# A block inversion in a delta-rule scan, moved from 64x64 blocks to 32x32 diagonal blocks on four tiles of TensorE

## The chip, the cores and the metric

One core of one Trainium2 chip runs one inference step of a hybrid backbone. The metric is device time in microseconds of one execution, the median of three runs. All data is float32 where nothing else is said.

## The reference, cut to what matters

384 tokens (128 of a prompt, 256 of a sample) go through a norm, a projection, two token mixers side by side (attention and a two-directional RWKV-7 scan), an output projection, and a mixture of 32 experts. The change touches the scan alone:

```
def step(S, xs):
    r_t, w_t, k_t, v_t, kk_t, a_t = xs
    sa = jnp.einsum("bhvk,bhk->bhv", S, kk_t)
    S = (S * w_t[:, :, None, :] - sa[..., None] * (kk_t * a_t)[:, :, None, :]
         + v_t[..., None] * k_t[:, :, None, :])
    return S, jnp.einsum("bhvk,bhk->bhv", S, r_t)
```

There are 8 heads of 64 channels and two directions, d = 0 (forwards) and d = 1 (backwards).

## The kernel before, in words

The scan is computed in chunks of HC = 64 tokens. A tile of 128 tokens holds two chunks, one in partitions 0 to 63 and one in 64 to 127. Within a chunk the recurrence is a unit triangular system of 64x64 for each head, and its inverse turns the recurrence into matmuls. Three pairs of (direction 0, direction 1) tiles are worked through one after the other; the pairs are numbered 0 to 2 here. Most work of the two directions is interleaved, and direction d owns the PSUM banks 4d to 4d+3, `bk(d, 0)` to `bk(d, 3)`.

For each pair the order is: decay and rate vectors, 32 transposes on TensorE, the Gram products (TensorE, 64x64 weights and 128 moving columns, out to all four banks), their masks into `AM` on VectorE (L1767), the product U = AM x values on TensorE (`quads` into bank 3), a piece of the attention branch's up-projection (`up_a`, 128x128 weights and 512 moving columns; two pieces in pair 0, one in pairs 1 and 2), then the inversion, then W and the product with the inverse (`s_u`), then the state steps and outputs.

The inversion keeps the inverse's transpose `XT` and the inverse `XM`, each [128, 8 heads, 64]. It starts from blocks of 2 (L1773, L1774, and the 32x32 block transposes of VectorE, L1776), and doubles the block in each of five levels, l = 1 to 5. A level is, for both directions: P = A x XM on TensorE, a masked copy of P into `PM` on VectorE (L1784), D = P x XT on TensorE, `XT` = `XT` - D on VectorE (L1788), and, in levels 1 to 4, a transpose of `XT` into `XM` (L1791). VectorE's transpose works in blocks of 32x32, which is enough up to level 4. TensorE's part is `quads`: 8 heads x 2 chunks = 16 matmuls with 64x64 weights and 64 columns, on the two diagonal 64x64 tiles of the array; a float32 matmul stands in the trace as two records on PE and two on PEld. `mm` (L719) and ScalarE's `cp` (L1243) are helpers through which most operations go.

After the last level, W (16 matmuls of 64x64, on all four 64x64 tiles) and another `quads` run on TensorE, ScalarE copies their banks (`WT`, `UV`), and VectorE computes the bonus products (L1793, L1794) and then `UU` (L1800 where a tile starts without a state, L1804 otherwise). The state steps wait for `UU`.

The work behind the scan (normalising, output projection, routing) waits for its last output, and SyncE's queue issues the experts' weights, in 1 MB pieces, once that is nearly through.

Of the kernel before, what the change touches and what calls it, by code (L numbers as in the profile page):

```python
# [74 lines left out]
HC = 64  # L75
NB = 3
# [27 lines left out]
def constants():  # L104
# [26 lines left out]
    lev = []  # L131
    for d in range(2):
        for l in range(LEVELS):
            same = (sm >> (l + 1)) == (ch >> (l + 1))
            tb, sb = (sm >> l) & 1, (ch >> l) & 1
            lev.append(same & ((sb == 0) & (tb == 1) if d == 0 else (sb == 1) & (tb == 0)))
    lev.append(sm == ch)
# [20 lines left out]
def build(nc, a, o):  # L158
    ctx = ExitStack()
    with ctx:  # L160
# [18 lines left out]
        level16 = sb("level16", [P, (2 * LEVELS + 1) * HC], U16)  # L179
        gramm = gram16[:, :].bitcast(BF16).rearrange("p (d n) -> p d n", d=2)  # L180
        levelm = level16[:, :].bitcast(BF16).rearrange("p (l n) -> p l n", n=HC)
# [71 lines left out]
        XM, XT = two(3072, HR, HC), two(3584, HR, HC)  # L253
# [3 lines left out]
        PM, GM, UV, UU = (two(6144 + i * DR, HR, HC) for i in range(4))  # L257
# [3 lines left out]
        S0D = two(6144, 4, HD)  # L261
# [95 lines left out]
        yc yo fin chain uud rsc gpn zfill chain2v qrm modrow condq routeq""".split()  # L357
# [56 lines left out]
        NP, NX = LEVELS - 1, 2 * LEVELS - 1  # L414
# [302 lines left out]
        def _(pe):  # L717
# [154 lines left out]

            def quads(out, l, r):

                for h in range(HR):
                    for b in range(2):
                        last = mm(out(h, b), l(h, b), r(h, b))
                return last
# [24 lines left out]
            bank_block = lambda bank: lambda h, b: bank[rows_of(b), h * HC:(h + 1) * HC]  # L903
            values_of = lambda j: lambda h, b: zbuf[rows_of(b), j, ZV + h * HD:ZV + (h + 1) * HD]

            for p, pair in enumerate(pairs):
# [49 lines left out]
                for d, j in pair:  # L956
                    pe.wait_ge(S["am"], 4 * (2 * p + d) + 4)
                    quads(bank_block(bk(d, 3)), blocks(AM[d], 2), values_of(j)).then_inc(s_u[d], 1)
# [12 lines left out]
                for l in range(1, LEVELS):  # L971
                    for d, j in pair:
                        pe.wait_ge(s_x[d], NX * p + 2 * l)
                        if l > 1:
                            pe.wait_ge(s_pc[d], NP * p + l - 1)
                        quads(bank_block(bk(d, 0)), blocks(AM[d], 0), blocks(XM[d])).then_inc(s_p[d], 1)
                    for d, j in pair:
                        pe.wait_ge(s_pc[d], NP * p + l)
                        quads(bank_block(bk(d, 2)), blocks(PM[d]), blocks(XT[d])).then_inc(s_d[d], 1)
# [262 lines left out]
        def _(sc):  # L1242
# [101 lines left out]
            for p, pair in enumerate(pairs):  # L1344
# [41 lines left out]
                for d, j in pair:  # L1386
                    sc.wait_ge(s_u[d], 3 * p + 2)
                    for b in range(2):
                        cp(WT[d][:, :, rows_of(b)], bk(d, b)[:, 0:4 * HC].rearrange("p (c t) -> p c t", c=4))\
                            .then_inc(s_uc[d], 1)  # L1390
                    sc.wait_ge(s_u[d], 3 * p + 3)
                    cp(flat(UV[d]), bk(d, 3)).then_inc(s_uc[d], 1)
# [108 lines left out]
        def _(ve):  # L1501
# [212 lines left out]
            idb = levelm[:, 2 * LEVELS:2 * LEVELS + 1, :].broadcast_to([P, HR, HC])  # L1714
            by_head = lambda bank: bank.rearrange("p (h t) -> p h t", h=HR)
            flat = lambda v: v.rearrange("p a b -> p (a b)")

            def both(first, second):
                first.then_inc(S["chain"], 1)
                chain[0] += 1  # L1720
                L(second)

            def start_state(p, d):

                k0 = 2 * chunk_of(0, d)
                tt(S0C[d], states[:, d, :, :], ecol[d][:, :, k0:k0 + 1].broadcast_to([P, 4, HD]), M).then_inc(S["s0p"], 1)

            for p, pair in enumerate(pairs):
# [41 lines left out]
                for d, j in pair:  # L1770
                    transposed = levelm[:, LEVELS * (1 - d):LEVELS * (1 - d) + 1, :].broadcast_to([P, HR, HC])
                    ve.wait_ge(S["am"], 4 * (2 * p + d) + 4)
                    L(tt(XT[d], AM[d][:, :, 0, :], transposed, M))  # L1773
                    tt(XT[d], idb, XT[d], SUB).then_inc(s_x[d], 1)  # L1774
                    ve.wait_ge(s_x[d], NX * p + 1)
                    ve.transpose(flat(XM[d]), flat(XT[d])).then_inc(s_x[d], 1)  # L1776

                for l in range(1, LEVELS):
                    for d, j in pair:
                        ve.wait_ge(s_p[d], NP * p + l)  # L1780
                        if l > 1:
                            ve.wait_ge(s_d[d], NP * p + l - 1)
                        m = levelm[:, LEVELS * d + l:LEVELS * d + l + 1, :].broadcast_to([P, HR, HC])
                        tt(PM[d], by_head(bk(d, 0)), m, M).then_inc(s_pc[d], 1)  # L1784
                    for d, j in pair:
                        ve.wait_ge(s_d[d], NP * p + l)
                        ve.wait_ge(s_x[d], NX * p + 2 * l)
                        tt(XT[d], XT[d], by_head(bk(d, 2)), SUB).then_inc(s_x[d], 1)  # L1788
                        if l < LEVELS - 1:
                            ve.wait_ge(s_x[d], NX * p + 2 * l + 1)  # L1790
                            ve.transpose(flat(XM[d]), flat(XT[d])).then_inc(s_x[d], 1)  # L1791

                both(*[tt(BON[d], KD[d], zr[d], M) for d in range(2)])  # L1793
# [356 lines left out]
```

## Time and profile before

| what | us |
|---|---|
| median of 3 runs | 1604.63 (1604.15 to 1606.7) |
| the profiled execution | 1607.96 |
| its span | 1606.1 |
| PE busy | 1451.2 |
| VectorE busy | 523.9 |
| scan, first pair's lora to the last output | about 275 to 478 |
| experts' loop, DMA share 1.01 | within 602 to 1560 |

A row of the timeline gives the start in the span, the time from the first start to the last end of a run of like instructions, the engine, the line and the operation. The distance from one start to the next is what bounds a run of matmuls, since they overlap: a run of n records with a duration of their own of 0.22 us and a length L has a mean distance of (L - 0.22)/(n - 1).

### The profile page before, as it was taken

Reading aid. Unit: us, or ns where it says so; the run is one execution under the profiler, and the core shown is the slowest. Engines: PE = TensorE matmul, PEld = TensorE weight load, DVE = VectorE, ACT = ScalarE, POOL = GpSimd, SP = SyncE. Lnnn points to the kernel's source line nnn. Section 1 sums busy time; section 2 is a strip of 40 time slices with the busy share of each in tenths; the row PEclk is TensorE's granted clock in tenths of the full one; section 3 lists DMA queues with packets and bytes.
Section 4 is the critical chain, followed back from the end, with each engine's and each line's share of the span. In section 5 each row is a group of like instructions: output and inputs, shape, how many; then the busy total and the mean of one; then the engine's idle time right before and its main releaser. Section 6 shows DMA issues by size and latency. Waiting matters only on the chain.

```text
span 1606.1 us, 26114 instructions
## 1 busy us (share of the span) xinstructions
PE 1451.2 (90%) x10008; PEld 690.7 (43%) x10009; DVE 523.9 (33%) x976; ACT 262.0 (16%) x514; POOL 100.1 (6%) x191
## 2 busy tenths in 40 slices
PE   4899998988977949999989999989999998998993
PEld 1677666677773443333323323323333332332331
DVE  3564644787887551111010111101101111010126
ACT  0332433231302110111110101101101111110110
POOL 1000000000001000000000000000000000000021
PEclk8899999999998959999999999999999999999997
DMA  9556835000017659999999999999999999999995
GB/s 363 207 178 242 342 125 199 2 3 10 25 48 247 245 227 403 421 421 422 421 422 421 421 422 420 422 421 421 422 421 421 422 421 421 421 421 415 421 406 189
DMA packets 97928, 510.78 MB, mean 318 GB/s; under 512 B 14752, under 2 KB 17072, under 8 KB 45160
## 3 DMA queue, kind: packets, MB, share of 16 engines
q1 hardware_dynamic: 82680, 480.08, 73.7%
q10 hardware_dynamic: 10336, 17.18, 2.9%
q0 software_dynamic: 4848, 12.59, 2.1%
q8 instruction: 50, 0.82, 0.2%
q14 instruction: 14, 0.11, 0.0%
HBM read 491.03 MB, written 22.71 MB: 320 GB/s over the span
## 4 chain that ended last, share of the span: by engine, by line
PE 64%; DMA 15%; DVE 10%; SPq 7%; issue 3%; ACT 1%; POOL 0%; DVEq 0%; ACTq 0%; POOLq 0%
PE bank L719 51%; PE bank L723 10%; SPq L596 6%; DMA ring<-w_moe_in 5%; DMA work<-w_moe_in 3%; DMA spare<-w_moe_in 3%; PE bank L726 3%; DMA zbuf<-w_ada 1%; DVE work L2068 1%; DMA work<-rows_d,dest 1%; DVE work L1788 1%; DVE work L1767 1%; DVE work L2069 1%; DVE work L1791 1%; ACT work L1243 1%
## 5 line engine op out<-in xcount | busy, mean ns | idle before, releaser
L719 PE MATMUL bank<-work 64*64 64x64 f32 (+3 forms) x5134 | 516.8, 353 | 34.8 <-DMA work<-w_moe_in 8.9
L719 PE MATMUL bank<-ring,work 128*64 128x512 f32 (+1 forms) x1376 | 353.2, 607 | 16.3 <-DMA ring<-w_moe_in 10.3
L719 PEld LDWEIGHTS bank<-work 64*64 64x64 f32 (+2 forms) x5134 | 233.8, 136 | 283.9 <-issue 232.0
L2062 DVE TENSOR_SCALAR work<-bank 128x512 f32<-128x512 f32 x39 | 27.0, 692 | 752.6 <-PE bank L719 752.6
L719 PEld LDWEIGHTS bank<-ring,work 128*64 128x64 f32 (+1 forms) x1376 | 115.4, 145 | 224.3 <-issue 192.6
L1243 ACT ACTIVATE work<-bank 128x512 f32<-128x512 f32 (+1 forms) x223 | 110.5, 513 | 540.9 <-PE bank L719 322.5
L723 PE MATMUL bank<-parts 128*128 128x512 f32 (+1 forms) x720 | 167.2, 386 | 2.9 <-DVE parts L449 2.9
L723 PEld LDWEIGHTS bank<-parts 128*128 128x128 f32 x720 | 128.5, 190 | 33.7 <-issue 5.2
L719 PE MATMUL bank<-zbuf,work 64*64 64x64 f32 (+2 forms) x966 | 126.8, 385 | 12.9 <-DMA zbuf<-w_moe_in 4.9
L1469 ACT ACTIVATE work<-work 128x512 f32<-128x512 f32 x39 | 24.6, 631 | 469.3 <-DVE work L2062 469.3
L719 PEld LDWEIGHTS bank<-zbuf,work 64*64 64x64 f32 (+2 forms) x966 | 55.5, 137 | 77.4 <-issue 59.7
L726 PE MATMUL bank<-ident,work 128*128 128x128 f32 (+1 forms) x340 | 67.1, 315 | 23.0 <-DVE work L2069 11.2
L449 DVE TENSOR_TENSOR parts<-ring,parts 128x1024 fp32r<-128x1024 f32 (+1 forms) x40 | 45.7, 1145 | 75.8 <-ACT parts L444 75.8
L726 PEld LDWEIGHTS bank<-ident,work 128*128 128x128 f32 (+1 forms) x340 | 47.6, 177 | 50.1 <-DVE work L2069 32.4
L719 PE MATMUL bank<-spare,work 128*64 128x512 f32 (+1 forms) x256 | 62.0, 563 | 3.2 <-ACT work L1243 2.2
L684 POOL TENSOR_TENSOR half<-half 128x1 f32<-128x1 f32 x38 | 7.0, 185 | 845.8 <-PE bank L726 832.9
L719 PE MATMUL bank<-first,work 128*64 128x512 f32 x208 | 53.0, 611 | 1.9 <-DMA first<-w_moe_in 1.9
L444 ACT ACTIVATE parts<-ring 128x1024 fp32r<-128x1024 f32 (+1 forms) x40 | 39.7, 994 | 76.4 <-PE bank L723 72.6
L2068 DVE TENSOR_SCALAR work<-bank 128x256 f32<-128x256 f32 x78 | 32.9, 421 | 56.7 <-PE bank L719 55.3
L671 POOL DMA_INDIRECT zbuf<-h_d,slots x39 | 41.0, 1052 | 19.8 <-issue 19.8
L719 PE MATMUL bank<-rowc 96*64 96x512 bf16 x234 | 39.9, 392 | 1.8 <-issue 1.8
L726 PEld LDWEIGHTS bank<-ident,zbuf 128*128 128x128 f32 x204 | 23.2, 148 | 37.6 <-issue 37.5
(264 smaller groups left out, 856.9 us busy)
## 6 DMA issues: line engine op xcount, KB each, us to landing
work<-w_moe_in SPq DMA_DIRECT2D x108, 1024.0 KB, 23.5
ring<-w_moe_in SPq DMA_DIRECT2D x84, 1024.0 KB, 25.5
work<-w_moe_out SPq DMA_DIRECT2D x64, 1024.0 KB, 21.0
ring<-w_moe_out SPq DMA_DIRECT2D x44, 1024.0 KB, 20.9
ring<-w_ada SPq DMA_DIRECT2D x11, 2048.0 KB, 7.4
zbuf<-w_moe_in SPq DMA_DIRECT2D x22, 1024.0 KB
first<-w_moe_in SPq DMA_DIRECT2D x21, 1024.0 KB
spare<-w_moe_in SPq DMA_DIRECT2D x21, 1024.0 KB, 23.2
```

The lines of the kernel that those rows point to most:

```text
L444: nc.scalar.activation(zpart(t, 0, n), z_quarter(t), ACT.Copy).then_inc(S["hi"], 1)
L449: eng.tensor_tensor(zpart(t, 1, n), z_quarter(t), zpart(t, 0, n), ALU.subtract)\
L596: sp.dma_start(place_of(turn_e, c), src).then_inc(s_place[(WC * turn_e + c) % NPLACE], 16)
L671: gp.indirect_dma_start(xg, None, h2_d.rearrange("t (h n) -> (t h) n", h=2), bass.IndirectOffsetOnAxis(ap=slots[:, 0:1], axis=0), bounds_c ...
L719: return pe.matmul(out, l, r, start=start, stop=stop)
L723: return pe.matmul(out, l, r, start=start, stop=stop, skip_group_check=True)
L726: return pe.transpose(out, src, ident[0:n, 0:n])
L1243: cp = lambda out, src, scale=1.0: sc.activation(out, src, ACT.Copy, scale=scale)
L1469: sc.activation(th, gl, ACT.Tanh, scale=ALPHA / 2).then_inc(S["thd"], 1)
L1767: tt(dst, bk(d, 2 * par + i).rearrange("p (c n) -> p c n", c=2), gramm[:, d:d + 1, :].broadcast_to([P, 2, 4 * HC]), M).then_inc(S["am"], 1)
L2062: ts(gl, B[0], LIMIT, None, ALU.min).then_inc(S["thd"], 1)
L2068: LL(ts(uu[:, seg], B[1][:, seg], LIMIT, -LIMIT, ALU.min, ALU.max))
```

## The change

The blocks of 32 are handled apart from the last doubling. The arrays of the inversion become [128, 8 heads, 32] (`XC`, `XM`, `PM`), with the four 32-token blocks of a tile in the four partition groups of 32. The four levels l = 1 to 4 are one loop on TensorE (`pe.Fori`) whose waits are computed from the loop's register; a burst is now `eighths`, 8 heads x 4 blocks = 32 matmuls of 32x32 weights and 32 columns, on the four diagonal 32x32 tiles. Ahead of each burst stands `hold`, a matmul with 128x32 weights and one column. The starting block comes from a second, small Gram product (`diagonal_gram`, 32 matmuls per direction) that leaves the diagonal blocks of all heads in two banks. The last level is written out as `across`: 16 matmuls of 32x32 for P and 16 for D, between the two blocks of a chunk; ScalarE copies P and writes the off-diagonal blocks of `XT` (two copies per direction), and VectorE fills the two diagonal blocks of `XT` with one masked copy.

```
+            def hold(bank):
+                mm(bank[0:32, 0:1], ident[:, 0:32], ident[:, 0:1])
+            def diagonal_gram(d):
+                for c in range(4):
+                    for par in range(2):
+                        r = rows_of(par)
+                        for q in range(4):
+                            last = mm(bk(d, 2 * par)[part(q), part(c)], BKT[d][r, 0, c, part(q)], QRT[d][r, c, 0, part(q)])
+                return last
+            def eighths(bank, l, r):
+                for h in range(HR):
+                    for q in range(4):
+                        last = mm(bank[part(q), part(h)], l(q, h), r[part(q), h, :])
+                return last
+            def across(bank, d, l, r, into):
+                for h in range(HR):
+                    for b in range(2):
+                        src, dst = 2 * b + (d if into else 1 - d), 2 * b + (1 - d if into else d)
+                        last = mm(bank[part(dst), part(h)], l(src, dst, h), r[part(src), h, :])
+                return last
...
                 for d, j in pair:
+                    pe.wait_ge(S["am"], 4 * (2 * p + d) + 2)
+                    diagonal_gram(d).then_inc(S["gdiag"], 1)
+                for d, j in pair:
                     pe.wait_ge(S["am"], 4 * (2 * p + d) + 4)
                     quads(bank_block(bk(d, 3)), blocks(AM[d], 2), values_of(j)).then_inc(s_u[d], 1)
...
-                for l in range(1, LEVELS):
+                with pe.Fori(0, SMALL - 1) as it:
                     for d, j in pair:
-                        pe.wait_ge(s_x[d], NX * p + 2 * l)
-                        if l > 1:
-                            pe.wait_ge(s_pc[d], NP * p + l - 1)
-                        quads(bank_block(bk(d, 0)), blocks(AM[d], 0), blocks(XM[d])).then_inc(s_p[d], 1)
+                        pe.wait_ge(s_x[d], 2 * it + (NX * p + 2))
+                        pe.wait_ge(s_pc[d], it + (NP * p + 1))
+                        hold(bk(d, 0))
+                        eighths(bk(d, 0), lambda q, h: AM[d][part(q), h, 0, part(q % 2)], XM[d]).then_inc(s_p[d], 1)
                     for d, j in pair:
-                        pe.wait_ge(s_pc[d], NP * p + l)
-                        quads(bank_block(bk(d, 2)), blocks(PM[d]), blocks(XT[d])).then_inc(s_d[d], 1)
+                        pe.wait_ge(s_pc[d], it + (NP * p + 2))
+                        hold(bk(d, 2))
+                        eighths(bk(d, 2), lambda q, h: PM[d][part(q), h, :], XC[d]).then_inc(s_d[d], 1)
+                for d, j in pair:
+                    pe.wait_ge(s_x[d], NX * p + 2 * SMALL)
+                    pe.wait_ge(s_pc[d], NP * p + SMALL)
+                    across(bk(d, 0), d, lambda src, dst, h: AM[d][part(src), h, 0, part(dst % 2)], XM[d], True).then_inc(s_p[d], 1)
+                for d, j in pair:
+                    pe.wait_ge(s_pc[d], NP * p + SMALL + 1)
+                    across(bk(d, 2), d, lambda src, dst, h: PM[d][part(src), h, :], XC[d], False).then_inc(s_d[d], 1)
...
                 for d, j in pair:
+                    sc.wait_ge(s_p[d], NP * p + SMALL)
+                    sc.wait_ge(s_d[d], NP * p + SMALL - 1)
+                    cp(flat(PM[d]), bk(d, 0)[:, 0:HR * QB]).then_inc(s_pc[d], 1)
+                for d, j in pair:
+                    sc.wait_ge(s_d[d], NP * p + SMALL)
+                    sc.wait_ge(s_x[d], NX * p + 2 * SMALL + 1)
+                    for b in range(2):
+                        r = slice(QB * (2 * b + d), QB * (2 * b + d + 1))
+                        cp(XT[d][r, :, QB * (1 - d):QB * (2 - d)], bk(d, 2)[r, 0:HR * QB].rearrange("p (h t) -> p h t", h=HR), -1.0)\
+                            .then_inc(s_x[d], 1)
...
-                        m = levelm[:, LEVELS * d + l:LEVELS * d + l + 1, :].broadcast_to([P, HR, HC])
+                        m = levelm[:, SMALL * d + l:SMALL * d + l + 1, :].broadcast_to([P, HR, QB])
                         tt(PM[d], by_head(bk(d, 0)), m, M).then_inc(s_pc[d], 1)
...
-                        tt(XT[d], XT[d], by_head(bk(d, 2)), SUB).then_inc(s_x[d], 1)
-                        if l < LEVELS - 1:
-                            ve.wait_ge(s_x[d], NX * p + 2 * l + 1)
-                            ve.transpose(flat(XM[d]), flat(XT[d])).then_inc(s_x[d], 1)
+                        tt(XC[d], XC[d], by_head(bk(d, 2)), SUB).then_inc(s_x[d], 1)
+                        ve.wait_ge(s_x[d], NX * p + 2 * l + 1)
+                        ve.transpose(flat(XM[d]), flat(XC[d])).then_inc(s_x[d], 1)
+                for d, j in pair:
+                    halves_of = XT[d].rearrange("p h (i t) -> p h i t", i=2)
+                    own_half = levelm[:, 2 * SMALL + 1:2 * SMALL + 3, :].unsqueeze(1).broadcast_to([P, HR, 2, QB])
+                    tt(halves_of, XC[d].unsqueeze(2).broadcast_to([P, HR, 2, QB]), own_half, M).then_inc(s_x[d], 1)
+
+                for d in range(2):
+                    ve.wait_ge(s_x[d], NX * p + 2 * SMALL + 1)
+                    ve.wait_ge(s_d[d], NP * p + SMALL)
```

## Rows read from the trace of the kernel before

**Rows 1.** The page: the queue that fetches instructions (packets, MB, share of 16 engines' span).

```profile
q8 instruction: 50, 0.82, 0.2%
```

**Rows 2.** Busy time by window: the inversions, what follows pair 0, routing, the experts.

```profile
core 0: us, PE busy (x) PEld busy (x) DVE busy (x) ACT busy (x) POOL busy (x), PEclk, DMA share, GB/s
305.00:342.00 37.00, 32.58 (x1071) 30.52 (x1071) 27.96 (x47) 3.00 (x7) 0.00 (x0) 1.00 0.01 4
345.00:358.00 13.00, 12.14 (x43) 6.52 (x44) 12.47 (x23) 6.63 (x14) 0.00 (x0) 0.87 0.01 2
562.00:602.00 40.00, 20.08 (x143) 17.15 (x141) 23.22 (x91) 4.89 (x11) 2.48 (x6) 0.58 0.60 229
620.00:1540.00 920.00, 879.51 (x4084) 304.19 (x4084) 113.52 (x226) 106.51 (x225) 57.03 (x146) 0.98 1.01 421
```

**Rows 3.** Timeline of levels 1 and 2 in pair 0, from level 1's first burst.

```profile
305.69 4.02 PE L719 MATMUL bank<-work 64*64 64x64 f32 x128
...
310.32 1.15 PE L719 MATMUL bank<-work 64*64 64x64 f32 x32 [0.60 <-DVE work L1791]
...
311.64 3.09 PE L719 MATMUL bank<-work 64*64 64x64 f32 x96 [0.17 <-DVE work L1791]
312.83 0.69 DVE L1784 TENSOR_TENSOR work<-bank,level 128x512 f32<-128x512 f32 x1 [0.63 <-PE bank L719]
313.77 0.69 DVE L1788 TENSOR_TENSOR work<-work,bank 128x512 f32<-128x512 f32 x1 [0.24 <-PE bank L719]
314.49 0.71 DVE L1791 STREAM_TRANSPOSE work<-work 128x512 f32<-128x512 f32 x1
315.12 0.65 DVE L1788 TENSOR_TENSOR work<-work,bank 128x512 f32<-128x512 f32 x1
315.26 1.15 PE L719 MATMUL bank<-work 64*64 64x64 f32 x32 [0.53 <-DVE work L1791]
315.81 0.71 DVE L1791 STREAM_TRANSPOSE work<-work 128x512 f32<-128x512 f32 x1
316.45 0.69 DVE L1784 TENSOR_TENSOR work<-bank,level 128x512 f32<-128x512 f32 x1
316.57 3.09 PE L719 MATMUL bank<-work 64*64 64x64 f32 x96 [0.17 <-DVE work L1791]
```

**Rows 4.** Timeline: operations of 128x256 on VectorE in pair 0's state steps.

```profile
340.18 0.42 DVE L1821 TENSOR_TENSOR work<-work,smallc 128x256 f32<-128x256 f32 x1
340.52 0.42 DVE L1816 TENSOR_TENSOR work<-bank,work 128x256 f32<-128x256 f32 x1
340.98 0.43 DVE L1821 TENSOR_TENSOR work<-work,smallc 128x256 f32<-128x256 f32 x1
```

**Rows 5.** Timeline of PE: a run on all four 64x64 tiles, and the next.

```profile
340.29 0.74 PE L719 MATMUL bank<-work 64*64 64x64 f32 x34
340.82 0.33 PE L719 MATMUL bank<-zbuf,work 64*64 64x64 f32 x4
```

**Rows 6.** Timeline of pair 1 from its Gram products to its first level.

```profile
360.89 3.72 PE L719 MATMUL bank<-work 64*64 64x128 f32 x128
362.13 4.88 DVE L1767 TENSOR_TENSOR work<-bank,gram 128x512 f32<-128x512 f32 x8 [2.00 <-PE bank L719]
...
364.68 1.15 PE L719 MATMUL bank<-zbuf,work 64*64 64x64 f32 x32
...
367.07 1.15 PE L719 MATMUL bank<-zbuf,work 64*64 64x64 f32 x32 [1.24 <-DVE work L1767]
...
368.14 3.70 PE L719 MATMUL bank<-ring,first 128*128 128x512 f32 x8
...
370.42 0.71 DVE L1776 STREAM_TRANSPOSE work<-work 128x512 f32<-128x512 f32 x1
...
371.68 1.04 PE L726 MATMUL bank<-ident,work 128*64 128x128 f32 x8
...
372.65 4.03 PE L719 MATMUL bank<-work 64*64 64x64 f32 x128
```

**Rows 7.** Timeline of pair 0 from level 5's first burst to UU.

```profile
325.13 1.15 PE L719 MATMUL bank<-work 64*64 64x64 f32 x32 [0.53 <-DVE work L1791]
...
329.59 0.69 DVE L1788 TENSOR_TENSOR work<-work,bank 128x512 f32<-128x512 f32 x1 [0.32 <-PE bank L719]
330.17 0.66 ACT L1243 ACTIVATE work<-bank 128x256 f32<-128x256 f32 x2 [23.77 <-PE bank L719]
...
332.84 0.88 DVE L1800 TENSOR_SCALAR work<-work 64x512 f32<-64x512 f32 x2
```

## The prediction on record

> **What bounds the kernel now.** I read the windows first [rows 2]. In the experts' loop the DMA share is 1.01 at 421 GB/s: that stage takes what its bytes take. The weights' queue is opened by the work behind the scan, so a microsecond gained or lost in the scan moves the whole loop and the end by one. In the windows of the scan the DMA share is 0.01 and neither PE nor VectorE is full (32.6 and 28.0 of 37 us): there the two wait for each other, and a price has to be read from the timeline.
>
> In the timeline of a level [rows 3] the first burst of a level starts at 310.32, then at 315.26: a period of 4.94. It is a ring. VectorE starts D of direction 0 at 313.77 and ends the transpose of direction 1 at 315.81 + 0.71 = 316.52: 2.75 us, four operations on 128x512. PE starts 0.05 later (316.57) with P of direction 1, then D of direction 0: the same two bursts started at 311.64, and their result is used at 313.77, so 2.13 for two, which is 2 x 0.94 and 0.25 of latency after the last. 2.75 + 0.05 + 2.13 = 4.93. PE waits 0.53 and 0.17 in this ring: it is near to being the bound. Level 1 takes 310.32 - 305.69 = 4.63. Four levels take 19.45 in a pair.
>
> **What VectorE saves.** All its operations of the inversion go from 128x512 to 128x256. Such operations take 0.42, 0.46 to a dependent one and 0.34 to an independent one [rows 4]. No transpose of 128x256 is in the trace; between nothing saved (0.71) and the same ratio I take the ratio, 0.44, since its 512 takes what an arithmetic one takes. The four operations become 0.46 + 0.36 + 0.44 + 0.44 = 1.70: 1.05 less in the ring.
>
> **What TensorE pays.** A burst goes from 16 matmuls to 32, that is from 32 PE records to 64, and before each stands `hold`. All turns on the distance between records, call it r. Quads run at (1.15 - 0.22)/31 = 30 ns on two tiles [rows 3], Gram products with 128 columns at (364.68 - 360.89)/128 = 29.6 ns on four [rows 6], and a run of 64 columns on four tiles at (340.82 - 340.29)/34 = 15.6 ns [rows 5]. Times the tiles that is 60, 118 and 62 ns for a record on its own tile: it goes with the columns. By that a record of 32 columns takes 30 to 35 ns on its tile, with four tiles in turn r = 8 to 9. But no row shows records closer than 15.6 ns, so whether they can be issued so close is unknown: the bounds are 7.5 (62/8) and 30 (no better than quads). I take 9, the tile's own time, as the 15.6 is itself explained by the tiles; a burst is then 64 x 9 = 0.58 instead of 0.94. A change from 64x64 to 128x128 work costs about 0.11 (last start at 368.00, next at 368.14, where the step had been 0.03) [rows 6]; I charge the same on the way back and 0.06 for `hold`'s own two records: 0.3 per burst, 0.15 where PE stood idle anyway (bounds 0.1 and 0.4).
>
> The Trainium skill (TensorE: Matmul & The Clock Gate, Back-to-back issue gap) puts a floor of about 25 ns under the distance of small matmuls. By it a burst would be 1.6 us and this change a loss; the 15.6 ns of the four-tile run disagrees with it.
>
> **The new ring.** 1.70 (VectorE) + 0.05 + 0.15 + 0.58 (P of direction 1) + 0.3 + 0.58 (D of direction 0) + 0.25 = 3.61. The loop's branch and its computed waits are in no row; below nothing, above one fetched block of instructions per turn, 0.2% x 16 x 1606 / 50 = 1.0 us [rows 1]; I take 0.1, since a block's code is there from the turn before. 3.71 against 4.94: -1.23, in levels 2 to 4: -3.7. Level 1 starts with all bursts in a row: 0.73 + 0.88 + 0.88, then 0.25, 0.90 of VectorE and 0.05: 3.69, with the branch 3.8 against 4.63: -0.8.
>
> **Ahead of the loop.** VectorE's starting blocks shrink from 2.1 us a direction to about 1.2, but that gains nothing: in pair 1 its last transpose is done at 371.13 and PE starts level 1 at 372.65, since it is busy with `up_a` and state transposes [rows 6]. PE does pay: the diagonal Gram of direction 1 waits for the sixth mask (362.13 + 6 x 0.61 = 365.8) and `quads` for U of direction 0, now done by 365.8 beside the masks, comes behind it. 0.05 + 64 records (0.6) + 0.95 + 0.95 ends at 368.4 to 368.6, against 368.0: +0.6 (bounds +0.3 and, at 30 ns, +1.9). Behind it wait `up_a` and the loop, so all of it shows.
>
> **The last level.** Before, from its first burst at 325.13 to W's start is about 4.2 (D of direction 0 is done at 329.27, as the other direction's follows at 329.59), and to `UU` 7.7 [rows 7]. After: P bursts of 32 records on two tiles (at 16 ns 0.5), copy by ScalarE (0.33 each [rows 7] and 0.25 of latency), D bursts (0.5), two copies of ScalarE: P of direction 1 starts at 0.85, ends 1.35, is copied at 1.95; D of direction 0 is out at about 2.05, its two copies at 2.7, W at 2.75. That is 1.4 sooner; at 30 ns per record 0.4. The bonus products of VectorE may start at 2.7, against 5.1, so they don't hold `UU` up. VectorE's copy of the diagonal halves (2 x 0.69) lies beside P and D. I take -1.2.
>
> **Sum.** 3 x (+0.6 - 0.8 - 3.7 - 1.2) = 3 x -5.1 = -15. Against the profiled execution, 1607.96 (1.9 us outside the span), that is 1593; it is 3.3 above the median of the runs, so for the median 1604.6 - 15 = 1590.
>
> **Rivals.**
> 1. TensorE becomes the bound, by the distance of its records. A burst costs C = 64 r + 0.3. Once C is over 1.2 (D of direction 1 is then longer than VectorE's way from D to the next P), the ring is 4 C. At r = 15.6, the closest row, C = 1.3 and the level 5.2, with the branch 5.3: +0.37 in three levels, +0.5 in level 1, +1.0 ahead, -1.0 at the end: +1.6 per pair, +5 in all, 1609. The sign turns at about 14.5 ns. For it: that row is the fastest there is, and 30 ns looks like a habit of all 64x64 runs. Against: each row is explained by columns over tiles. In the middle, at 12 ns: C = 1.07, ring 1.2 + 3.2 + 0.1 = 4.5, and with the rest about -2 per pair, 1598.
> 2. The four tiles of a burst don't overlap because all four row groups write to one bank. Serially a record of 512 columns takes 0.44 (8 in 371.68 - 368.14) [rows 6], 0.86 ns per column, so 32 columns 28 ns: a burst of 1.8, C = 2.1, a level 8.5, 3.6 over today's: with level 1 (+3.8) and the prelude (+1.9) some +16 per pair, +47, 1650. Against it: two row groups of `quads` share a bank and run at 30 ns, where serial work would need 55.
> The Trainium skill (TensorEngine Tiling (Array Packing), Restrictions and Gotchas) says that different row tiles cannot access the same PSUM bank simultaneously; it would give this rival, and by the 30 ns of `quads` the trace does not agree.
> 3. The loop's edge costs a fetched block each time: 1.0 instead of 0.1 on 12 turns [rows 1], +11: about 1601, little or no change. Against it: the experts' loop fetches next to nothing and runs at the DMA's pace.
> 4. The granted clock falls. It is 1.00 in the inversions, 0.87 after the state steps and 0.58 in routing, where PE is busy half of the time [rows 2]. PE stays busy for 3 of 3.7 us in the new ring, so I give it little; at half clock a tile's record takes twice as long, r = 17, and a level 5.6: +10, 1614.
>
> **How the numbers follow.** No change is within 0.2% of the median, 3.2 us, about what a measurement of this kernel can tell. r up to about 10.5: 0.50 (1584 to 1594, faster). r of 11 to 13.5: 0.15 (1594 to 1601, mostly faster). r of 14 to 16: 0.15 (1602 to 1610, same or slower). One bank, or a floor of 25 ns or more (a level of 7.6, +36): 0.08. The loop's edge: 0.07, same or slightly faster. Clock: 0.05. Faster 0.62, same 0.13, slower 0.25. The range takes in the first three and the third rival: 1583 to 1609; the likeliest case alone spans 1584 to 1594.
>
> **What the changed profile would show.** Burst to burst: `eighths` as 64 records of 32*32 in 0.6 to 0.8 us, with a `hold` of 128*32 about 0.15 before; a run of 1.0 or 1.9 means rival 1 or 2. VectorE's masks at 0.42 and its transposes at 0.44. A level period of 3.7; PE idle before P of direction 0 and of direction 1 for 0.1 to 0.4 (none: PE is the bound). `up_a` 0.6 later behind the masks. W of each pair about 5 us sooner after its Gram. A stage behind the scan with the same lengths, and experts' weights issued 15 us sooner. The prediction fails if records of 32x32 keep 14.5 ns or more, if the transposes don't shrink (+0.6 a level at most), or if each turn of the loop stalls.

## The result, and the profile after

The changed kernel takes 1618.1 us (median of 7 runs, 1613.05 to 1624.99) against 1604.63 (7 runs, 1603.75 to 1606.7): ratio 1.0084, 95% interval 1.0060 to 1.0109. It is slower by 0.8%, and outside the range that was given. Its runs also spread four times as wide, and the longer ones have the lower mean granted clock (0.938 at 1613.05, 0.930 at 1624.99). The profiled execution took 1618.1, its span is 1616.1 (before: 1606.1). The medians are 13.5 us apart and the spans only 10.0, mostly because before's profiled execution lay 3.3 us above its own median.

The page after: span, instructions, clock by slice, and the queue that fetches instructions ([rows 1] before: 50 packets). A packet is 0.77 MB / 47, 16 KB.

```profile
span 1616.1 us, 30228 instructions
...
PEclk7799999888967968999999999999999999999997
...
q8 instruction: 47, 0.77, 0.2%
```

TensorE and VectorE in pair 0, from level 1's first burst on, which answers to [rows 3]:

```profile
308.04 0.22 PE L723 MATMUL bank<-ident 128*32 128x1 f32 x2
...
308.19 0.75 PE L723 MATMUL bank<-work 32*32 32x32 f32 x64
...
308.88 0.22 PE L723 MATMUL bank<-ident 128*32 128x1 f32 x2
308.99 0.42 DVE L1843 TENSOR_TENSOR work<-bank,level 128x256 f32<-128x256 f32 x1 [7.75 <-PE bank L723]
...
310.70 0.44 PE L723 MATMUL bank<-work 32*32 32x32 f32 x29
311.12 0.45 DVE L1849 STREAM_TRANSPOSE work<-work 128x256 f32<-128x256 f32 x1
...
312.97 0.74 PE L723 MATMUL bank<-work 32*32 32x32 f32 x35 [1.83 <-issue]
...
313.86 0.26 PE L723 MATMUL bank<-ident 128*32 128x1 f32 x2
...
314.05 1.07 PE L723 MATMUL bank<-work 32*32 32x32 f32 x64
```

Three things are to be seen. A burst at first is what was forecast: 64 records in (0.75 - 0.22)/63 = 8.4 ns each. In the fourth burst, after 29 of its 64 records, TensorE stands still for 1.83 us and waits for nothing that a semaphore shows. And behind the stop the same burst takes 1.07 instead of 0.75. The windows of the same stretch (columns as in [rows 2]; the clock is the number ahead of the DMA share) say why: the granted clock has gone to 0.50, the 1.2 GHz level.

```profile
308.00:310.00 2.00, 2.00 (x151) 1.83 (x153) 0.60 (x2) 0.60 (x1) 0.00 (x0) 1.00 0.00 0
310.00:312.00 2.00, 1.14 (x95) 0.97 (x90) 1.12 (x3) 0.00 (x0) 0.00 (x0) 1.00 0.04 8
312.00:314.00 2.00, 0.88 (x37) 0.76 (x37) 0.25 (x1) 0.00 (x0) 0.00 (x0) 0.53 0.00 0
314.00:316.00 2.00, 2.00 (x124) 1.91 (x127) 1.04 (x3) 0.00 (x0) 0.00 (x0) 0.50 0.00 0
...
334.00:336.00 2.00, 2.00 (x60) 2.00 (x58) 1.22 (x2) 0.97 (x3) 0.00 (x0) 0.50 0.00 0
336.00:338.00 2.00, 2.00 (x76) 1.98 (x71) 0.55 (x2) 1.44 (x4) 0.00 (x0) 1.00 0.03 8
```

It stays there for 24 us, with TensorE busy nearly all the time. The other two pairs show the same: a stop in the fourth burst of the loop's first turn, and half the clock behind it (380.4 to 390.6 and again 397.4 to 400.9 in pair 1, 445.2 to 472.5 in pair 2). Their stops:

```profile
381.28 0.43 PE L723 MATMUL bank<-work 32*32 32x32 f32 x13 [2.20 <-issue]
...
448.14 0.87 PE L723 MATMUL bank<-work 32*32 32x32 f32 x48 [4.21 <-issue]
```

The levels of pair 1, where the clock comes back just ahead of the last turn: a level of 391.83 - 386.95 = 4.88, mostly at 1.2 GHz, and one of 395.40 - 391.83 = 3.57 at 2.4 GHz.

```profile
386.95 0.26 PE L723 MATMUL bank<-ident 128*32 128x1 f32 x2 [0.18 <-issue]
...
391.83 0.22 PE L723 MATMUL bank<-ident 128*32 128x1 f32 x2 [0.36 <-DVE work L1849]
...
395.40 7.58 PE L723 MATMUL bank<-work 32*32 32x32 f32 x272 [0.16 <-DVE work L1849]
```

The second fall in pair 1 comes without a stop. From 391.0 to 397.4 the clock is at 1.00, TensorE is busy for 5.74 of 6.40 us, and it waits for 0.36 us at most. In the levels before it is busy for 12.71 of 15 us (310 to 325) and the clock stays at 1.00.

```profile
392.00:394.00 2.00, 2.00 (x174) 1.89 (x175) 1.23 (x3) 0.00 (x0) 0.00 (x0) 1.00 0.00 0
394.00:396.00 2.00, 1.84 (x143) 1.65 (x129) 1.52 (x5) 0.00 (x0) 0.00 (x0) 1.00 0.00 0
396.00:398.00 2.00, 1.86 (x92) 1.68 (x88) 1.35 (x3) 1.26 (x4) 0.00 (x0) 0.86 0.00 0
```

Where the time went, change against before in us, by the starts of the parts in the two timelines (level 1 is from its first burst to level 2's; the last level from its first burst to `UU`):

| part | forecast, 3 pairs | pair 0 | pair 1 | pair 2 | measured, sum |
|---|---|---|---|---|---|
| prelude: first mask to first burst | +1.8 | +1.3 | +0.4 | +1.0 | +2.7 |
| level 1 | -2.4 | +1.2 | +1.5 | +3.6 | +6.3 |
| levels 2 to 4 | -11.1 | +0.1 | -1.3 | -0.1 | -1.3 |
| last level to `UU` | -3.6 | -0.2 | -1.0 | +1.7 | +0.5 |
| ahead of the masks and behind `UU` | 0 | +0.6 | -1.3 | -0.2 | -0.8 |

But for rounding the sum is +7.3, and the scan went from 200.7 to 208.0. With +1.3 ahead of the scan and +2.6 between the scan and the experts' weights (there too products run at the lower clock), the weights are issued 11.2 later and the span is 10.0 longer. In pair 1 before has a dip of the clock at 347 to 350, which after does not have; its masks start 1.6 sooner behind the pair's start, and that is the -1.3.

### The profile page after: what moved, and what is told of

It reads as the page before. It is cut to its first block, busy times and chain, and to the rows that moved or that the text cites. A ratio compares the mean times of both kernels' runs of the same rounds, so it can differ in the third digit from the quotient of the medians.

```text
span 1616.1 us, 30228 instructions
## 1 busy us (share of the span) xinstructions
PE 1462.3 (90%) x12024; PEld 700.7 (43%) x12025; DVE 497.5 (31%) x976; ACT 268.6 (17%) x532; POOL 99.8 (6%) x191
## 4 chain that ended last, share of the span: by engine, by line
PE 65%; DMA 15%; SPq 8%; DVE 7%; issue 3%; ACT 1%; POOL 0%; DVEq 0%; ACTq 0%; POOLq 0%
PE bank L723 52%; PE bank L727 10%; SPq L600 7%; DMA ring<-w_moe_in 5%; DMA spare<-w_moe_in 3%; DMA work<-w_moe_in 3%; PE bank L730 3%; DMA zbuf<-w_ada 1%; DVE work L2133 1%; DMA work<-rows_d,dest 1%; DVE work L2134 1%; DVE work L1824 1%; ACT work L1286 1%; DVE ring L2146 0%; DMA rows_d<-work 0%
## 5 line engine op out<-in xcount | busy, mean ns | idle before, releaser
L723 PE MATMUL bank<-work 32*32 32x32 f32 (+5 forms) x7054 | 522.9, 322 | 35.2 <-issue 8.3
L723 PEld LDWEIGHTS bank<-work 32*32 32x32 f32 (+4 forms) x7054 | 233.9, 138 | 283.1 <-issue 242.1
L1286 ACT ACTIVATE work<-bank 128x256 f32<-128x256 f32 (+3 forms) x241 | 117.4, 502 | 550.0 <-PE bank L723 325.5
```

What stands on the lines that cost most here:

```text
L723: return pe.matmul(out, l, r, start=start, stop=stop)
L1286: cp = lambda out, src, scale=1.0: sc.activation(out, src, ACT.Copy, scale=scale)
```

## The experiments

Two theories for the stop: F, the code isn't there (it comes in blocks, and TensorE uses them up faster than they arrive), against L, the loop's branch and computed waits. Two for the clock: G, the stop alone makes it fall and it takes its time, against H, the 32x32 work does not keep the clock up or bring it back, stop or not.

**1. Levels written out.**

```
-                with pe.Fori(0, SMALL - 1) as it:
+                for it in range(SMALL - 1):
```

> The changed kernel with its four equal levels written out instead of a loop on TensorE, nothing else. In the changed kernel PE stood still for 1.83, 2.20 and 4.21 us in the fourth burst of the first turn of each loop, 458 to 502 instructions after its head. Theory F (the code arrives in blocks of 16 KB, 256 instructions, and PE, which now uses one up in 1.2 us, outruns it): written out, every block is outrun, 8 blocks a pair at some 3 us each, levels of 6 us or more, no faster than the changed kernel: 1618 to 1630 us. Rival L (the loop's branch or its register waits cause the stop): no stops in the bursts, and some 3 us less per pair: 1605 to 1610 us.

Measured: 1643.4 us, ratio 1.0243 (1.0226 to 1.0260). TensorE in pair 0:

```profile
312.12 0.47 PE L723 MATMUL bank<-work 32*32 32x32 f32 x34 [1.56 <-issue]
...
315.82 0.75 PE L723 MATMUL bank<-work 32*32 32x32 f32 x39 [1.33 <-issue]
...
319.55 0.84 PE L723 MATMUL bank<-work 32*32 32x32 f32 x43 [1.12 <-issue]
...
323.53 0.86 PE L723 MATMUL bank<-work 32*32 32x32 f32 x48 [1.38 <-issue]
...
327.26 0.95 PE L723 MATMUL bank<-work 32*32 32x32 f32 x52 [1.12 <-issue]
```

From one resumption to the next there are 126 to 128 matmul records, so with their weight loads about 256 instructions, and in these rows 3.7 to 4.0 us (3.3 to 4.1 over the three pairs, once 5.2). Without a stop the same number of records takes 2.3 us at half clock, since a burst with its `hold`, 66 records, takes 1.20. A packet of 16 KB over 256 instructions is 64 bytes for each. This is F: code comes in blocks of 256 instructions, one per some 3.7 us, which is 14.5 ns per instruction and 29 ns per record as the closest spacing that a long stretch of such code kept. `quads` of 64x64 at 30 ns per record [rows 3] just doesn't outrun it. L is refuted: without a loop the waits of this kind between 300 and 510 us are 28, 30.2 us in all, against 12 and 10.4 with it. The size was missed: 1618 to 1630 was expected.
By the Trainium skill (Runtime: NRT & Kernel Launch, Instruction fetch mechanics) code comes in 16 KiB blocks of 256 instructions, which these rows bear out. The Trainium skill says in the same section that the fetch is hidden by the sequencer's own pace; the stops of 1.1 to 1.6 us show that this does not hold here.

**2. The loop's code moved against the blocks.** The loop's head is put at slot 210 of a block.

```
-                with pe.Fori(0, SMALL - 1) as it:
+                with nc.Fori(0, SMALL - 1, engines=[mybir.EngineType.PE], head_slot={mybir.EngineType.PE: 210}) as it:
```

> The changed kernel with the loop's first instruction put at slot 210 of a block of 256, so that the body (about 550 instructions) crosses a block's edge 46, 302 and 558 instructions in: the first crossing is made while PE's queue still works on the up-projection, and the third is not reached. Theory F: the stop in the first turn goes or shrinks below 0.5 us in all three pairs, 8 us in all. For the clock, which was 0.50 for 24, 10 and 27 us after these stops: theory G (a stop lets the clock fall) expects 1.00 throughout and levels of 3.6 us, in all 1588 to 1595 us; theory H (bursts on 32x32 tiles do not keep the clock up by themselves) expects it to fall all the same and 1605 to 1612 us. Rival L expects the stops to stay where they are.

Measured: 1615.74, ratio 1.0088 (1.0057 to 1.0118), no different from the changed kernel. The stop moved with the code: in every pair it now stands behind 15 of the 64 records of the third burst, about where the expectation had the second edge (302 instructions in). It is shorter, 1.15, 1.40 and 1.84 us, but not below 0.5 as was expected:

```profile
308.90 0.62 PE L723 MATMUL bank<-work 32*32 32x32 f32 x49 [1.15 <-issue]
```

F again for the place, with the size missed. The clock is still at 0.50 from 311 to 335 in pair 0, and for 17.1 and 23.9 us in the others (10.2 and 27.3 in the changed kernel): a shorter stop spared little or nothing of that, and the time is above both that were expected.

**3. The loop and `hold` alone, at 64x64.** The kernel before, with all its five levels as one loop and `hold` ahead of each burst.

```
-                for l in range(1, LEVELS):
+                with pe.Fori(0, LEVELS - 1) as it:
...
+                        hold(bk(d, 0))
                         quads(bank_block(bk(d, 0)), blocks(AM[d], 0), blocks(XM[d])).then_inc(s_p[d], 1)
```

> The kernel before with its five levels as one loop on TensorE, with the same computed waits and a hold ahead of each burst, all on 64x64 tiles as it was. Theory F: a body of 272 instructions at 15 ns each takes a block in 3.8 us, so no stop above 0.3 us; the hold costs 0.45 in each ring of 4.94, about +7 us in 15 levels: 1609 to 1613 us, clock 1.00. Rival L: stops of 2 us in each first turn and a clock of 0.5 behind them: 1620 us or more.

Measured: 1612.24, ratio 1.0062 (1.0045 to 1.0079), as expected.

```profile
310.21 0.22 PE L719 MATMUL bank<-ident 128*32 128x1 f32 x2 [0.38 <-DVE work L1798]
...
311.44 0.22 PE L719 MATMUL bank<-ident 128*32 128x1 f32 x2
...
315.59 0.22 PE L719 MATMUL bank<-ident 128*32 128x1 f32 x2 [0.39 <-DVE work L1798]
```

A burst with its `hold` takes 1.23 where `quads` alone takes 0.94, so `hold` and the two changes of shape cost 0.3, as the prediction charged, and the ring is 5.38 instead of 4.94. No stop and no loss of clock anywhere in the levels: the loop does neither.

**4. A stop without 32x32 work.** The kernel before, in which VectorE repeats a masked copy in level 1 two, three and six times, so that TensorE waits 1.31, 2.04 and 4.21 us in pairs 0, 1 and 2.

```
+                        if l == 1 and d == 0:
+                            for _ in range((2, 3, 6)[p]):
+                                L(tt(PM[d], by_head(bk(d, 0)), m, M))
                         tt(PM[d], by_head(bk(d, 0)), m, M).then_inc(s_pc[d], 1)
```

> The kernel before (64x64 bursts, no loop), with VectorE repeating the first masked copy of level 1 two, three and six times in pairs 0, 1 and 2, so that PE stands still for about 1.4, 2.2 and 4.3 us in level 1; what is computed is the same. Theory G (a stop lets the clock fall, whatever the matmuls): the clock goes to 0.50 after at least the two longer stops. Theory H (it is the 32x32 work that does not hold or regain the clock): here, with 64x64 bursts behind, it stays at 1.00 or is back within 5 us, against 10 to 27 us in the changed kernel. Time: 7.5 us of stops and what the clock costs, 1612 to 1620 us.

Measured: 1613.3 (one run). The windows of pair 1:

```profile
376.00:378.00 2.00, 0.09 (x2) 0.09 (x4) 1.93 (x4) 0.00 (x0) 0.00 (x0) 1.00 0.61 131
378.00:380.00 2.00, 2.00 (x52) 2.00 (x54) 1.17 (x3) 0.00 (x0) 0.00 (x0) 0.69 0.00 0
380.00:382.00 2.00, 2.00 (x42) 1.99 (x40) 1.69 (x3) 0.00 (x0) 0.00 (x0) 0.50 0.03 8
382.00:384.00 2.00, 2.00 (x66) 1.93 (x64) 1.44 (x3) 0.00 (x0) 0.00 (x0) 0.96 0.00 0
```

1.31 us did nothing to the clock. Behind 2.04 and towards the end of 4.21 it fell, and with 64x64 work to follow it was low for 3.4 us each time (378.7 to 382.1, 447.0 to 450.4). So a stop can start the fall (G), but a stop of 4.21 us did not make it last the 27 us that it lasted behind one of the same length in pair 2 of the changed kernel. And the stop of 1.15 in experiment 2, shorter than the 1.31 here, had a low clock behind it for 23.9 us.

**5. No stop, with 32x32 work.** The changed kernel, whose bursts read the upper 16 bits of each number as bfloat16: half the instructions per burst, and products that are not the reference's.

```
-                        last = mm(bank[part(q), part(h)], l(q, h), r[part(q), h, :])
+                        last = mm(bank[part(q), part(h)], top(l(q, h)), top(r[part(q), h, :]))
```

```profile
310.00:312.00 2.00, 1.35 (x102) 1.17 (x102) 1.68 (x5) 0.00 (x0) 0.00 (x0) 1.00 0.00 0
312.00:314.00 2.00, 1.27 (x93) 0.93 (x77) 1.87 (x6) 0.00 (x0) 0.00 (x0) 0.82 0.00 0
314.00:316.00 2.00, 1.72 (x102) 1.42 (x102) 1.58 (x4) 0.00 (x0) 0.00 (x0) 0.50 0.00 0
```

The clock is at 0.50 for 13.7 us in pair 0 and for 17.1 and 13.7 in pairs 1 and 2, behind waits of at most 0.7 us in pair 0's levels, such as the levels before also have [rows 3]. That agrees with H, but does not show it by itself: this kernel has half the records too, and TensorE is busy for only 2.62 of the 4 us around the fall (310 to 314), where no 4 us of the levels before have less than 3.30. The second fall in pair 1 of the changed kernel, with TensorE busy for 5.74 of 6.40 us, does not leave that way out. The scan takes 182.7 us, 18 less than before, in spite of the clock; of the 18, 12.4 are seen in the span. How much of it is the code and how much TensorE's halved work is not separated.

**6. The changed kernel with wide products in each turn.** Nothing moved; four extra 128x128x128 products per turn into a bank that nobody reads, which the result doesn't need, and one wait ahead of the loop until that bank is free.

```
+                    for k in range(4):
+                        mm(bk(0, 3)[:, 0:P], ident[:, :], ident[:, :], k == 0, k == 3)
```

> The changed kernel with nothing moved, and in each turn of the loop, behind the two P bursts, four extra products of 128x128x128 (identity by identity) into a bank that nobody reads: work that no result needs. The first pass's stop for code stays. Theory H (the 32x32 work does not keep the granted clock up or bring it back, wide products do): after the stop the clock is back at 1.00 within about 5 us, as in the kernel with slices; the ring is then 4.7 to 4.9 at full clock against 5.05 at half clock in the changed kernel, and the last level and W run at full clock: 1613 to 1618 in spite of 1.1 us more work a turn. Rival (the stop alone sets how long the clock is down): it stays at 0.50 for 10 to 20 us as before, the slice costs 2 us at half clock and the ring is over 6: 1630 or more.

Measured: 1616.33, ratio 1.0062 (1.0040 to 1.0083).

```profile
318.00:320.00 2.00, 2.00 (x130) 1.91 (x127) 0.86 (x2) 0.00 (x0) 0.00 (x0) 0.52 0.00 0
320.00:322.00 2.00, 1.78 (x145) 1.57 (x133) 1.29 (x3) 0.00 (x0) 0.00 (x0) 1.00 0.00 0
```

The clock is down for 6.8 us instead of 23.9 in pair 0, for 3.4 instead of 10.2 in pair 1 and for 6.8 instead of 27.3 in pair 2, and then stays up to the end of the loop; the ring at full clock is 325.13 - 320.32 = 4.81. With 1.2 us more work in each turn the kernel is as fast as without it. The stops are shorter too in pairs 0 and 1 (0.81 + 0.40 and 1.00), but 3.69 against 4.21 in pair 2. H, not the stop alone. Two things were missed: "about 5" was written for the 6.8, and the last level was to run at full clock, where the clock fell once more in pairs 1 and 2 (398.6 and 470.2), for 3.4 us each.

**7. Useful wide work in each turn.** In place of the extra products the second unit of the up-projection, in slices of 128 columns, one per turn, behind the two P bursts, so it is gone from the prelude. The second kernel of this kind also has the loop's head at slot 20.

```
-                    up_a(0, 1, bk(1, 1))
...
+                    up_slice(p, it, bk(1, 1) if p == 0 else bk(0, 1))
```

> The changed kernel with the up-projection piece that stood ahead of the loop (one unit of 512 columns per pair) cut into four slices of 128 columns, one slice per turn of the loop, between P and D of the two directions: the same matmuls, 0.86 us of 128x128 work in each turn. Theory F: the stop in the first turn shrinks by about 0.9 us. Theory G: it still drops the clock if over 1 us is left. Theory H: the slices keep the clock at 1.00 outside a stop. If the clock stays up, a level is 4.3 us, the loop starts 3.4 us sooner in each pair, and the time is 1590 to 1598 us; if it falls, 1612 to 1620 us.

Measured: 1607.39, ratio 1.0022 (1.0004 to 1.0040): the best of the 32x32 kernels that compute the whole result. It lies between the two times that were expected for a clock that stays and one that falls, as the clock did one in pair 0 and the other in pairs 1 and 2.

```profile
315.78 0.22 PE L723 MATMUL bank<-ident 128*32 128x1 f32 x2 [0.36 <-DVE work L1851]
...
317.45 1.16 PE L723 MATMUL bank<-ring,first 128*128 x8
...
320.60 0.22 PE L723 MATMUL bank<-ident 128*32 128x1 f32 x2 [0.32 <-DVE work L1851]
```

In pair 0 the stop is 0.29 us and the clock 1.00 to its end; the ring of 4.82 includes 1.09 for the slice, and the pair takes 64.7 us against 68.1 before. Pairs 1 and 2 still have stops of 1.58 and 0.81 + 0.95 with a low clock of 3.4 and 6.8 us behind them, and the last level with W, where no slice stands, loses the clock in pair 2 (459.5 to 466.3) and has a stop of 1.99 there.

> The variant with the up-projection's slices in the loop, its loop head put at slot 20 of a code block, so that the block edges lie 236 and 492 instructions into the body, with a slice between them. Theory F: the way from one edge to the next takes 2.9 us against some 3.7 us for a block to come, so a stop of about 0.8 us in each pair at the same place, against 0.3 to 2.0 us; the clock stays up in the loops; 1598 to 1605 us. Rival L: no effect of the place.

Measured: 1612.0, ratio 1.0049 (1.0032 to 1.0066). Expected were 1598 to 1605, stops of about 0.8 and a clock that stays up in the loops: a miss in all three. The stops are 1.01, 1.56 and 2.15 + 1.27: no better place for the head. And the clock was low for 3.4, 10.2 and 10.2 us, with a slice in each turn. So wide work in the loop went with shorter falls than the 23.9, 10.2 and 27.3 of the changed kernel, but it did not prevent them or bound them at a few us.

**8. The last level's copies on VectorE.** The kernel with slices and slot 20; VectorE copies both P and writes the off-diagonal blocks of direction 1.

```
-                    cp(flat(PM[d]), bk(d, 0)[:, 0:HR * QB]).then_inc(s_pc[d], 1)
...
+                    ve.wait_ge(s_p[d], NP * p + SMALL)
+                    ve.wait_ge(s_d[d], NP * p + SMALL - 1)
+                    cp(flat(PM[d]), bk(d, 0)[:, 0:HR * QB]).then_inc(s_pc[d], 1)
```

> The same, and the last level's copies dealt anew: VectorE instead of ScalarE copies P of both directions and writes the off-diagonal blocks of direction 1, ScalarE those of direction 0, and ScalarE's copy of the up-projection lies ahead of them. The last level, from the last transpose to UU, was 6.5 us in the changed kernel (6.45 in the kernel before). If it is bound by ScalarE's chain, it gets 0.5 to 1 us shorter per pair, 2 to 3 us in all, 1596 to 1602 us; if by TensorE's W and product, nothing changes.

Measured: 1616.49, ratio 1.0079 (1.0049 to 1.0108), where 1596 to 1602 was expected. A miss; its interval overlaps that of the kernel it starts from. In pair 0:

```profile
327.79 0.42 DVE L1851 COPY work<-bank 128x256 f32<-128x256 f32 x1 [0.41 <-PE bank L723]
328.13 1.28 DVE L1855 TENSOR_TENSOR work<-work,level 128x512 f32<-128x512 f32 x2
328.91 0.77 ACT L1290 ACTIVATE work<-bank 32x256 f32<-32x256 f32 x2 [3.89 <-DVE work L1855]
329.62 0.88 DVE L1862 TENSOR_SCALAR work<-bank 32x256 f32<-32x256 f32 x2 [0.20 <-DVE work L1855]
```

The 1.28 us of diagonal blocks, which lay beside P and D, now stand behind the P copies, and the off-diagonal blocks on both engines wait for them: W starts 3.61 us behind the level's first burst instead of 3.24. `UU` of direction 0 comes at 7.19 instead of 5.60, but most of that is not the copies: the clock is at 0.50 from 328.6 to 335.4, which pair 0 of the kernel with slot 20 does not have.

**9. The slices without the 32x32 work.** The kernel before, its levels written out and 64x64, with half of that unit (four slices of 64 columns) or all of it (four of 128, as in this edit) behind D of direction 1 in levels 1 to 4.

```
                         quads(bank_block(bk(d, 2)), blocks(PM[d]), blocks(XT[d])).then_inc(s_d[d], 1)
+                    if l <= 4:
+                        last = up_part(p, later, 0 + (l - 1) * 128, 128)
```

> The kernel before with its 64x64 levels written out, and nothing of the 32x32 work. Of the second unit of the up-projection, half (256 columns) stays ahead of level 1; the rest is cut into four slices of 64 columns, one behind D of direction 1 in levels 1 to 4, where TensorE stands idle for 0.53 and 0.17 us a level. Theory (the idle time of TensorE in a level can hold other work, and level 1 starts as soon as the prelude's TensorE work ends): a slice is 8 records of 64 columns, about 0.45 to 0.55 us and 0.1 to 0.2 for the change of shape, so 0.6 to 0.75 against 0.70 of idle time: a level stays 4.9 to 5.0. Level 1 starts 1.8 us sooner in pair 0 and 1.5 sooner in pairs 1 and 2 (there VectorE's last transpose holds it): -4 to -5 in all, about 1600 us, ratio 0.997. Rival (the idle time is used by latency that a slice delays): a level gets 0.3 longer or more, and the gain is under 1.5 us, no difference from 1604.6. The granted clock stays at 1.00 in both.

> As the kernel with slices of 64 columns, but the whole unit is moved: nothing of it ahead of level 1, four slices of 128 columns. A slice took 1.09 us in the 32x32 kernel with slices, 0.4 more than a level's idle time of 0.70, so a level is 5.3. Pair 0 starts level 1 3.5 us sooner and pays 1.6 back; pairs 1 and 2 start 1.5 sooner and pay 1.6 back: -2 in all, about 1603 us. Rival: a level stays under 5.0 and pair 0 keeps 3.5, in all -6, 1599.

Measured: 1602.87, ratio 0.9986 (0.9970 to 1.0001), and 1605.13, ratio 0.9985 (0.9968 to 1.0002): no difference that can be told from none. TensorE with slices of 64, then of 128 columns:

```profile
307.54 1.10 PE L719 MATMUL bank<-ring,first 128*128 128x64 f32 x8
308.57 4.04 PE L719 MATMUL bank<-work 64*64 64x64 f32 x128
312.55 1.10 PE L719 MATMUL bank<-ring,first 128*128 128x64 f32 x8
```

```profile
306.54 1.16 PE L719 MATMUL bank<-ring,first 128*128 128x128 f32 x8
307.62 4.02 PE L719 MATMUL bank<-work 64*64 64x64 f32 x128
311.58 1.16 PE L719 MATMUL bank<-ring,first 128*128 128x128 f32 x8
```

A slice costs 1.03 with 64 columns (0.6 to 0.75 was expected) and 1.08 with 128: the price goes by the 8 records with their 128x128 weights, not by the columns. The level is 5.01 and 5.04, so the idle time took all but 0.1 of it: by starts there were 4.94 - 3.8 = 1.1 us free, more than the 0.53 and 0.17 of the rows, which begin only where the last record's own 0.22 ends. Pair 0 went from 68.1 to 66.3 and 64.9, pair 1 from 67.2 to 65.9 and 65.0. Pair 2 gained nothing: it had stops of 2.26 and 1.04 us in its state steps, for which no semaphore shows either; that they are for code was not tried. The gain in the pairs was expected at 4 to 5 and 2 us; it was 0.8 and 5.3 in the profiled scans, and neither can be made out in the medians.

## Why the prediction was wrong

**What held.** The disputed number, the distance of records on four tiles in one bank, is 8.4 ns (9 was taken); rivals 1 and 2 are out. That it came out does not show the reason that was given, a tile's own time: by that reason the distance would double at half clock (17 in rival 4), and it went to 12.7. What sets the 8.4 stays open. VectorE's operations take 0.42 and its transpose 0.45 (0.42 and 0.44). A burst with `hold` is 0.83 to 0.84 from start to start (0.88). The ring at full clock is 3.57 (3.61 without the branch). The scan's loss went through to the end, as [rows 2] said.
The two rules of the Trainium skill that the prediction weighed (TensorE: Matmul & The Clock Gate, Back-to-back issue gap; TensorEngine Tiling (Array Packing), Restrictions and Gotchas) would have given 25 ns or more; the 8.4 ns do not agree with either.

**The step that failed first** is the loop's edge in the new ring: "I take 0.1, since a block's code is there from the turn before". That is true of turns 2 to 4 (0.18 at half clock, nothing at full clock). In the first turn it isn't there: TensorE uses 458 instructions in 3.1 us (308.04 to 311.14) and the blocks come one per 3.7. Rival 3 had the fetch, but per turn and with a packet's time at the DMA engines (1.0 us), not the time until the next block is there. Price: the stops, 1.83 + 2.20 + 4.21 = 8.2 us. In pair 2 the packet goes beside `w_out`, 2 MB that SyncE issues when the last `up_a` is done and that take 8.9 us to land; at a DMA share of 0.99 the stop is about twice as long. This is what the prelude and level 1 show as +9.0 instead of -0.6. That it was the code is shown (experiments 1 to 3); that `w_out` lengthened the stop is read from this window, the 3.69 of experiment 6 and the 1.84 of experiment 2 in the same pair, where the others had 1.15 and 1.40, and wasn't tried by moving it.

```profile
446.00:448.00 2.00, 0.00 (x0) 0.00 (x0) 0.00 (x0) 0.00 (x0) 0.00 (x0) 0.50 0.99 371
```

**The second failed step** is rival 4, the clock: "PE stays busy for 3 of 3.7 us in the new ring, so I give it little". Busy time did not bring the clock back: it is at 0.50 in windows with TensorE busy for 2.00 of 2.00 us. Nor did it hold it: in pair 1 the clock fell at 397.4 with TensorE busy for 5.74 of the 6.40 us before. Its mechanism and its price were nearly right (a level of 5.6 forecast, 5.04 measured; a record 12.7 ns, not 17), only its chance of 0.05 was not. At half clock TensorE is the bound: four times 1.20 from `hold` to `hold`, and a level is no shorter than before's 4.94. Of the nine levels 2 to 4 one ran wholly at full clock. So -11.1 became -1.3. Experiments 4 to 6 show that both the stop and the kind of work have a part; to which of the two a fall behind a stop is owed can't be said of the changed kernel.

**The third term**, the last level (-1.2 a pair), came out at -0.2, -1.0 and +1.7, but at half clock: nearly all of the level in pair 0, all of it in pair 2, and 3.4 us of it in pair 1. In the kernel of experiment 7, pair 0, at full clock, it takes 330.86 - 325.26 = 5.60 from its first burst to `UU` of direction 0, against 7.7 [rows 7]: -2.1; `UU` of direction 1 comes 1.2 sooner. So the term was no smaller than forecast, and was lost to the clock.

**Forecast at the clock that the change leaves itself** would have been: prelude and level 1 +3 a pair, levels 2 to 4 nothing, the last level nothing, some +9; the run shows +10 in the span.

## What to carry to other kernels

Price a run of small TensorE instructions in instructions too: here it did not go on faster than some 256 per 3.7 us for longer than the code at hand, so halving a tile and doubling the count buys speed only in code that is already there, and the first pass of a loop isn't. Ask of the clock what kind of work holds it, not only how much of the time is busy; a level that is bound by TensorE at the lower clock is worth computing before a chance is given. And an independent wide product can be cut into slices for the idle time of a ring: by starts the idle time is larger than its rows say, and in the 32x32 kernels the low clock was mostly shorter with it. In the kernel before it gained nothing that the medians show.

## What the hardware showed that wasn't expected

Four 32x32 tiles that write to one bank take records 8.4 ns apart. The granted clock was 0.50 for 24 us with TensorE busy nearly throughout on 32x32 and then 64x64 tiles, while with 64x64 work behind stops of 2.0 and 4.2 us it was low for 3.4, and a stop of 1.3 us did not move it. It also fell under 32x32 work with no wait above 0.36 us. In pair 1 it did come back by itself after 10 us of 32x32 work; why there and not in the others stays open. Code arrived one block of 256 instructions per 3.3 to 4.1 us, and a written-out sequence of 32x32 products stood still at every block from the first stop on.
